# Seven block products for the up projection of MLP groups 2 to 4, and weight sums made in a memory scratch

## The chip, the cores and the metric

One core of a Trainium2 chip runs the kernel. The metric is the device time of one execution in microseconds (us). Its engines are TensorE (PE), which multiplies matrices and loads their stationary side (PEld); VectorE (DVE); ScalarE (ACT); GpSimd (POOL); and SyncE (SP), which here only issues transfers (DMA).

## The reference

One decoder layer on 512 tokens of width 1024. Three branches (a short convolution, a gated linear recurrence, attention into 256 memory tokens) are gated, merged, projected and added to the input; then comes the MLP that this change is about. All in float32:

```
x = layer_norm(ALPHA * x + mixed, ln1_g, ln1_b)
h = square(relu(x @ w_up))                                       # 512 x 4096
x = layer_norm(ALPHA * x + h @ w_down, ln2_g, ln2_b)             # w_up 1024 x 4096, w_down 4096 x 1024
```

## The kernel before

Every product of float32 operands is made of three matmuls (`three`, lines 1767 to 1771): each operand is split into a high part, a rounded copy that ScalarE makes, and a low part, the difference, that VectorE makes (`low_of`, line 1069); then high by high, high by low and low by high are added in a bank. Weights come in slabs of 1 MB (128 x 2048 floats), which SP loads. A slab's high part goes to one of four slots of `w_hi` and its low part to `w_lo`; `slab_hi` and `slab_lo` count them, and TensorE waits for `slab_lo` before it uses a slab.

The MLP works in 4 groups of 1024 hidden features. In a group, TensorE first makes 8 up tiles (`up_tile`) of 128 features by 512 tokens, each from all 8 row blocks of x. ScalarE takes a tile out of its bank with relu and square in its two token halves, and VectorE makes from a pair of tiles the operands of the down projection. That one is a 2 x 2 block product (2 blocks of 256 tokens, 2 blocks of hidden features, 2 blocks of outputs) done in seven products instead of eight. The products m1 to m7 multiply sums of blocks of h (the forms, `h_forms`, `form_hi`, `form_lo`) by blocks of w_down or sums of them. VectorE makes those sums (`sum_of`, line 1591) in `raw_a`, `raw_b` and `raw_c`, parts of the tensor `small`. Each product has two rows, for 128 of the 256 tokens, of 12 matmuls of 512 columns. The products m1, m6, m7 and m4 accumulate one after the other in one pair of banks and m5 and m3 in another; after each of them VectorE adds the bank as it then stands to the residual (`down_add`), and the next product of the bank waits for that (`down_ready`).

In front of the MLP the gates of branches 2 and 3 already use seven products with columns of 256 tokens (`seven_product`, `SEVEN`, with the sums in `gate_a`, `gate_b`, `gate_c`), with a ring of three slots. `gate_a` lies in the memory of the fourth slot of `w_hi`, `gate_b` in that of `w_lo`.

Each engine works through an order written out by hand: `mlp`, `seven_gate` and `plain_gate` on ScalarE and VectorE, the list of loads on SP. GpSimd does little: in each of the two projection halves it splits the memory keys and values of that half (lines 613 to 615), then it clears `merged` (line 633), scales the residual (line 637) and shares in the last normalization. It issues no transfer. Each of its instructions waits for those ahead of it.

Of the kernel before, what the change touches and what calls it, by code (L numbers as in the profile page):

```python
# [24 lines left out]
P = 128  # L25
T = 512
# [28 lines left out]
S_MLP, N_MLP = S_OUT + 4, 11  # L55
# [21 lines left out]
UP_SLABS = 4  # L77
# [5 lines left out]

SHARED = ((2, 0), (2, 1), (3, 0), (3, 1), (0, 0))
# [3 lines left out]
LAST_ROWS = (("m3", 0), ("m2", 0), ("m3", 1), ("m2", 1), ("m7", 0), ("m4", 0), ("m7", 1), ("m4", 1))  # L88


def made(g, name, r):

    at = 2 * PRODUCTS.index(name) + r
    if g == G_MLP - 1 and (name, r) in LAST_ROWS:
        at = 2 * len(PRODUCTS) - len(LAST_ROWS) + LAST_ROWS.index((name, r))
    return 2 * len(PRODUCTS) * g + at + 1


SUMS = ("m5", "m6", "m7", "m4")


def aside(g, name):

    return g == G_MLP - 1 and name == "m2"
# [39 lines left out]
def down_bank(g, name):  # L144
    return 2 if g == G_MLP - 1 and name == "m4" else DOWN_BANK[name]


def down_slab(g, name):
    return S_MLP + g * N_MLP + UP_SLABS + PRODUCTS.index(name)

# [34 lines left out]
def build(nc, x, mem, lower_bounds, w_in, conv_w, hg_norm_w, w_mem_k, w_mem_v, w_branch, b_gate, w_o,  # L185
          ln1_g, ln1_b, w_up, w_down, ln2_g, ln2_b, out):
    ds = bass.ds
    with ExitStack() as ctx:
# [49 lines left out]
        h_forms = two[:, 4:6, :].rearrange("p a (b t) -> p (a b) t", t=T // 2)[:, 0:7, :]  # L238
# [19 lines left out]
        form_of = dict(m7=gate_a[:, 0:1024], m6=gate_a[:, 1024:2048], m5=gate_b[:, 0:1024], m3=gate_b[:, 1024:2048])  # L258
        small = sb("small", [P, 9 * 1024])
# [18 lines left out]
        raw_a = small[:, 0:SLAB]  # L278
        raw_b = small[:, SLAB:2 * SLAB]
        raw_c = small[:, 2 * SLAB:3 * SLAB]  # L280
        late = small[:, 8192:9216].rearrange("p (c t) -> p c t", t=256)
        early = two[:, 4, :].rearrange("p (c t) -> p c t", t=256)
        h_kept = small[:, 8192:9216].rearrange("p (j t) -> p j t", j=PAIRS)
        aside_hi, aside_lo = (t[:, 0:PAIRS, :].rearrange("p k c -> p (k c)") for t in (x_hi, x_lo))
# [51 lines left out]
        a_landed, b_landed = sem("a_landed"), sem("b_landed")  # L336
        c_landed, sums_made = sem("c_landed"), sem("sums_made")
        up_done, up_read = sem("up_done"), sem("up_read")
        h_squared, form_step, forms_made = sem("h_squared"), sem("form_step"), sem("forms_made")
        forms_hi, forms_ready = sem("forms_hi"), sem("forms_ready")  # L340
        kept_hi, kept_ready = sem("kept_hi"), sem("kept_ready")
        down_done, down_read = sem("down_done"), sem("down_read")
# [23 lines left out]

        def main_of(eng, rnd, t):

            eng.wait_ge(tile_done, rnd * MAIN + (t + 1))
            return bank[t % MAIN]  # L370
# [19 lines left out]
        wdn = w_down[0].rearrange("(k two p) c -> p two k c", two=2, p=P)  # L390

        def down_block(g, k, n):

            return wdn[:, k - 1, g * PAIRS:(g + 1) * PAIRS, (n - 1) * WID:n * WID]
# [14 lines left out]

        def direct_slab(g, d):  # L410

            return S_MLP + g * N_MLP + d if d < UP_SLABS else down_slab(g, "m2")

        @block.sync
        def _(sp):
# [116 lines left out]
            sp.wait_ge(gate_done, seven_done(2, "m6", 1))  # L532
            par_load(2, ln2_g)
            par_load(3, ln2_b)
            def direct(g, d, src, k):

                n = R_MLP + 5 * g + d
                if n < R_MLP + 2:
                    sp.wait_ge(slab_lo, S_MLP - 2 + d + 1)
                else:  # L540
                    before = 5 * g + d - 2
                    sp.wait_ge(slab_lo, direct_slab(before // 5, before % 5) + 1)
                sp.dma_start(raw[:, n % 2, :].rearrange("p (k c) -> p k c", k=k), src).then_inc(slab_landed[n % 2], 16)

            def up_load(g, j):
                direct(g, j, wup[:, :, g * D + j * 256:g * D + (j + 1) * 256], KD)

            for g in range(G_MLP):
                up_load(g, 0)
                up_load(g, 1)  # L550
                if g == 0:
                    sp.wait_ge(merged_split, KD)
                else:
                    sp.wait_ge(slab_lo, down_slab(g - 1, "m4") + 1)
                sp.dma_start(as_block(raw_a), down_block(g, 1, 1)).then_inc(a_landed, 16)
                if g:
                    sp.wait_ge(sums_made, 4 * g)
                sp.dma_start(as_block(raw_b), down_block(g, 2, 2)).then_inc(b_landed, 16)
                if g == 0:
                    sp.wait_ge(x1_ready, 2 * TB)  # L560
                else:
                    sp.wait_ge(slab_lo, down_slab(g - 1, "m7") + 1)
                sp.dma_start(as_block(raw_c), down_block(g, 1, 2)).then_inc(c_landed, 16)
                up_load(g, 2)
                up_load(g, 3)
                direct(g, 4, down_block(g, 2, 1), PAIRS)
# [17 lines left out]
        def _(pool):  # L584
# [25 lines left out]

            for half in range(2):
# [40 lines left out]
        def _(act):  # L652
# [282 lines left out]

# [17 lines left out]
            def split(s, src):  # L953
                act.activation(w_hi[:, (s - S_MLP) % 4, :], src, ACT.Copy).then_inc(slab_hi, 1)  # L954
# [1279 lines left out]
```

## Time and profile before

| what | us |
|---|---|
| median of three runs | 821.65 (821.57 to 821.92) |
| the profiled execution, its own time | 821.65 |
| its span, first to last instruction | 819.9 |
| granted TensorE clock, mean of the span | 0.997 |
| TensorE matmul busy | 809.6 |
| VectorE busy | 552.2 |
| ScalarE busy | 373.2 |
| GpSimd busy | 32.7 |
| moved by DMA | 87.64 MB |

A matmul's record begins when it enters the array and overlaps the next ones, so the distance between two starts is what one costs, and its duration is longer. The start of a weight slab's use can be told by the operand names: x_hi in an up tile, y_hi (where the forms lie) in a down row, x_forms in the gates' products.

### The profile page before, as it was taken

Reading aid. Unit: us, or ns where it says so; the run is one execution under the profiler, and the core shown is the slowest. Engines: PE = TensorE matmul, PEld = TensorE weight load, DVE = VectorE, ACT = ScalarE, POOL = GpSimd, SP = SyncE. Lnnn points to the kernel's source line nnn. Section 1 sums busy time; section 2 is a strip of 40 time slices with the busy share of each in tenths; the row PEclk is TensorE's granted clock in tenths of the full one; section 3 lists DMA queues with packets and bytes.
Section 4 is the critical chain, followed back from the end, with each engine's and each line's share of the span. In section 5 each row is a group of like instructions: output and inputs, shape, how many; then the busy total and the mean of one; then the engine's idle time right before and its main releaser. Section 6 shows DMA issues by size and latency. Waiting matters only on the chain.

```text
span 819.9 us, 10644 instructions
## 1 busy us (share of the span) xinstructions
PE 809.6 (99%) x4347; PEld 699.2 (85%) x4347; DVE 552.2 (67%) x612; ACT 373.2 (46%) x435; POOL 32.7 (4%) x40
## 2 busy tenths in 40 slices
PE   8999999999999999999999999999999999999995
PEld 8889888899888889989988899888888888888884
DVE  4647655477358628778567676985588568856887
ACT  5559324493435324443453036643554355435532
POOL 1100100000001000000000010000000000000006
PEclk9999999999999999999999999999999999999998
DMA  9641313313120730620547116028102710270002
GB/s 309 205 155 52 103 52 102 102 51 102 51 78 26 255 103 1 223 86 1 207 153 255 53 51 207 1 75 288 48 1 81 278 52 1 90 270 1 1 0 104
DMA packets 64207, 87.64 MB, mean 107 GB/s; under 512 B 1661, under 2 KB 43686, under 8 KB 64166
## 3 DMA queue, kind: packets, MB, share of 16 engines
q1 hardware_dynamic: 64166, 87.06, 31.4%
q8 instruction: 30, 0.49, 0.2%
q14 instruction: 11, 0.09, 0.0%
HBM read 84.96 MB, written 2.10 MB: 106 GB/s over the span
## 4 chain that ended last, share of the span: by engine, by line
PE 98%; DVE 1%; DMA 1%; issue 0%; SPq 0%; DVEq 0%
PE bank L1769 31%; PE bank L1771 31%; PE bank L1770 31%; DMA two<-in_mem_dram 1%; PE bank L1796 0%; PE bank L1985 0%; PE bank L1935 0%; PE bank L2105 0%; PE bank L1906 0%; PE bank L1988 0%; PE bank L1973 0%; PE bank L1937 0%; DVE smx L1637 0%; PE bank L1942 0%; DVE two L1631 0%
## 5 line engine op out<-in xcount | busy, mean ns | idle before, releaser
L1769 PE MATMUL bank<-x_hi,w_hi 128*128 128x512 f32 (+1 forms) x672 | 245.7, 366 | 0.0
L1770 PE MATMUL bank<-x_lo,w_hi 128*128 128x512 f32 (+1 forms) x672 | 244.6, 364 | 0.0
L1771 PE MATMUL bank<-x_hi,w_lo 128*128 128x512 f32 (+1 forms) x672 | 244.5, 364 | 0.0
L1771 PEld LDWEIGHTS bank<-x_hi,w_lo 128*128 128x128 f32 x672 | 126.8, 189 | 20.1
L1769 PEld LDWEIGHTS bank<-x_hi,w_hi 128*128 128x128 f32 x672 | 126.8, 189 | 19.7
L1770 PEld LDWEIGHTS bank<-x_lo,w_hi 128*128 128x128 f32 x672 | 126.9, 189 | 19.6
L1769 PE MATMUL bank<-w_hi,y_hi 128*128 128x512 f32 x296 | 115.5, 390 | 0.0
L1771 PE MATMUL bank<-w_hi,y_lo 128*128 128x512 f32 x296 | 115.2, 389 | 0.0
L1770 PE MATMUL bank<-w_lo,y_hi 128*128 128x512 f32 x296 | 115.2, 389 | 0.0
L1070 DVE TENSOR_TENSOR w_lo<-raw,w_hi 128x2048 fp32r<-128x2048 f32 (+2 forms) x35 | 71.5, 2046 | 36.2 <-ACT w_hi L954 26.3
L1771 PEld LDWEIGHTS bank<-w_hi,y_lo 128*128 128x128 f32 x296 | 55.6, 188 | 11.6
L1770 PEld LDWEIGHTS bank<-w_lo,y_hi 128*128 128x128 f32 x296 | 55.6, 188 | 11.4
L1769 PEld LDWEIGHTS bank<-w_hi,y_hi 128*128 128x128 f32 x296 | 55.6, 188 | 11.3
L1070 DVE TENSOR_TENSOR w_lo<-small,w_hi 128x2048 fp32r<-128x2048 f32 (+1 forms) x28 | 59.9, 2138 | 3.6 <-ACT w_hi L680 1.7
L954 ACT ACTIVATE w_hi<-raw 128x2048 fp32r<-128x2048 f32 x17 | 32.6, 1918 | 63.6 <-PE bank L1771 35.4
L1065 DVE TENSOR_TENSOR w_lo<-raw,w_hi 128x2048 fp32r<-128x2048 f32 x22 | 50.4, 2296 | 16.0 <-ACT w_hi L659 15.8
L954 ACT ACTIVATE w_hi<-small 128x2048 fp32r<-128x2048 f32 x24 | 45.7, 1906 | 10.2 <-PE bank L1771 10.2
L1631 DVE TENSOR_TENSOR two<-two,bank 128x512 f32<-128x512 f32 x56 | 38.3, 684 | 15.8 <-PE bank L1771 10.2
L659 ACT ACTIVATE w_hi<-raw 128x2048 fp32r<-128x2048 f32 x22 | 42.2, 1919 | 12.4 <-DMA raw<-in_w_branch_dram 11.4
L1769 PE MATMUL bank<-y_hi,w_hi 128*128 128x512 f32 (+1 forms) x128 | 46.9, 367 | 0.0
L1770 PE MATMUL bank<-y_lo,w_hi 128*128 128x512 f32 (+1 forms) x128 | 46.4, 363 | 0.0
L1771 PE MATMUL bank<-y_hi,w_lo 128*128 128x512 f32 (+1 forms) x128 | 46.4, 362 | 0.0
(252 smaller groups left out, 1145.3 us busy)
## 6 DMA issues: line engine op xcount, KB each, us to landing
raw<-in_w_in_dram SPq DMA_DIRECT2D x22, 1024.0 KB, 5.1
raw<-in_w_up_dram SPq DMA_DIRECT2D x16, 1024.0 KB, 6.9
small<-in_w_down_dram SPq DMA_DIRECT2D x12, 1024.0 KB, 7.8
raw<-in_w_branch_dram SPq DMA_DIRECT2D x6, 1024.0 KB, 5.1
two<-in_x_dram SPq DMA_DIRECT2D x4, 1024.0 KB, 9.2
raw<-in_w_o_dram SPq DMA_DIRECT2D x4, 1024.0 KB, 5.1
raw<-in_w_down_dram SPq DMA_DIRECT2D x4, 1024.0 KB, 4.7
small<-in_w_mem_v_dram SPq DMA_DIRECT2D x4, 512.0 KB, 10.9
```

Of the source, the lines that this page charges most:

```text
L659: act.activation(w_hi[:, slot, :], raw[:, r, :], ACT.Copy).then_inc(slab_hi, 1)
L954: act.activation(w_hi[:, (s - S_MLP) % 4, :], src, ACT.Copy).then_inc(slab_hi, 1)
L1065: dve.tensor_tensor(w_lo[:, slot, :], raw[:, r, :], w_hi[:, slot, :].bitcast(F32), ALU.subtract)\
L1070: return dve.tensor_tensor(dst, src, high.bitcast(F32), ALU.subtract)
L1631: dve.tensor_tensor(z, z, bank[down_bank(g, name) + r], op).then_inc(down_read, 1)
L1769: pe.matmul(dst, a[0], b[0], start=first, stop=False, skip_group_check=goes_on)
L1770: pe.matmul(dst, a[0], b[1], start=False, stop=False, skip_group_check=goes_on)
L1771: return pe.matmul(dst, a[1], b[0], start=False, stop=last, skip_group_check=goes_on)
```

## The change

The up projection of groups 2 to 4 becomes seven block products as well: 2 blocks of x's features, 2 blocks of hidden features, 2 blocks of 256 tokens. Group 1 keeps its plain tiles, and during it VectorE makes the forms of x (`x1_forms`) once for all groups. Every up product is 48 matmuls of 256 columns in a pair of banks. ScalarE copies m1, m5 and m6 out, VectorE adds m3, m2 and m7 to the copies, and relu and square follow on whole blocks of h. The blocks of h are 1024 columns wide (`h11`, `h12`, `h21`, `h22`), and the forms of the down projection are made on them with one operation each (`form`) instead of in four column parts. The down products run in the order m1, m2, m5, m6, m3, m7, m4.

VectorE makes no weight sums any more. GpSimd copies four blocks of the weights into a scratch in memory (`kept`) for each of seven jobs (the down projection of each group, the up projection of groups 2 to 4), and then adds block to block there with accumulating transfers, four per job. SP loads the sums like weights. The first four jobs are begun and summed in the projection halves, behind GpSimd's splitting of the memory values, and the other three after the clearing of `merged`. All MLP slabs run in one ring of three slots (`mlp_load`, `mlp_hi`, `mlp_lo`), whose third raw buffer is `gate_a`; a group has 14 slabs (the first 11). The rows of the second normalization are loaded in the last group instead of ahead of the MLP.

```diff
+ROWS = ("m1", "m2", "m5", "m6", "m3", "m7", "m4")
+ROW_BANK = dict(m1=6, m6=6, m7=6, m4=6, m2=4, m5=0, m3=0)
+UP_BANK = dict(m1=0, m6=0, m7=0, m4=0, m5=2, m3=2, m2=4)
+SUM_STEPS = (("m5", "m7"), ("m7", "m6"), ("m6", "m5"), ("m4", "m6"))
+JOBS = (("down", 0), ("up", 1), ("down", 1), ("up", 2), ("down", 2), ("up", 3), ("down", 3))
 # SyncE
+            def mlp_load(n, src, k):
+                if n < 2:
+                    sp.wait_ge(slab_lo, S_MLP - 2 + n + 1)
+                elif n == 2:
+                    sp.wait_ge(tile_done, mlp_round(0) * MAIN)
+                else:
+                    sp.wait_ge(slab_lo, S_MLP + n - 3 + 1)
...
+            def product_load(kind, g, name):
+                n = up_slab(g, name) if kind == "up" else down_slab(g, name)
+                if name in SUMS:
+                    j = JOBS.index((kind, g))
+                    sp.wait_ge(kept_made[j], KEPT)
+                    mlp_load(n, kept_sum(j, name), PAIRS)
...
 # GpSimd
+            def begin_sums(jobs):
+                for j in jobs:
+                    kind, g = JOBS[j]
+                    for name in SUMS:
+                        k, n = SUM_BEGINS[name]
+                        pool.dma_start(kept_sum(j, name), up_block(g, k, n) if kind == "up" else down_block(g, k, n))\
+                            .then_inc(kept_made[j], 16)
+            def make_sums(jobs):
+                for n, (to, other) in enumerate(SUM_STEPS):
+                    for j in jobs:
+                        pool.wait_ge(kept_made[j], 16 * (len(SUMS) + n))
+                        pool.dma_start(kept_sum(j, to), kept_sum(j, other), accum_op=ALU.add, max_dma_last_dim=8192)\
+                            .then_inc(kept_made[j], 16)
...
                 parts(mem_v[:, :, half * 256:(half + 1) * 256], mv_hi, mv_lo, 2 * half + 2, vhalf_ready)
+                if half == 0:
+                    pool.wait_ge(x_landed[1], 16)
+                    pool.wait_ge(value_landed[3], 16)
+                    begin_sums(range(0, 4))
+                else:
+                    make_sums(range(0, 4))
             pool.wait_ge(branch_split, 8)
             pool.memset(merged, 0.0).then_inc(merge_done, 1)
+            begin_sums(range(4, 7))
+            make_sums(range(4, 7))
 # ScalarE
+            def mlp_hi(n):
...
+                elif n > 2:
+                    act.wait_ge(mlp_done, slab_done(n - 3, 1))
+                mlp_landed(act, n)
+                act.activation(w_hi[:, n % 3, :], mlp_raw(n), ACT.Copy).then_inc(slab_hi, 1)
 # VectorE
+            def down(g):
+                last = g == G_MLP - 1
+                form(g, "m5")
+                form(g, "m7")
+                mlp_lo(down_slab(g, "m5"))
+                form_to_lo(g, "m5")
+                form(g, "m6")
+                form(g, "m3")
+                mlp_lo(down_slab(g, "m6"))
+                form_to_lo(g, "m6")
+                down_add(g, "m1", 0)
+                down_add(g, "m1", 1)
+                form_to_lo(g, "m3")
+                mlp_lo(down_slab(g, "m3"))
+                down_add(g, "m5", 0)
+                down_add(g, "m5", 1)
+                mlp_lo(down_slab(g, "m7"))
+                form_to_lo(g, "m7")
+                for r in range(2):
+                    down_add(g, "m2", r)
...
                 down_add(g, "m6", 0)
                 down_add(g, "m6", 1)
+                mlp_lo(down_slab(g, "m4"))
+                form_to_lo(g, "m4")
...
                 down_add(g, "m3", 0)
                 down_add(g, "m3", 1)
+                down_add(g, "m7", 0)
+                mlp_lo(up_slab(g + 1, "m1"))
+                down_add(g, "m7", 1)
+                mlp_lo(up_slab(g + 1, "m5"))
+                down_add(g, "m4", 0)
+                down_add(g, "m4", 1)
 # TensorE
+            def up_product(g, name):
+                n = up_slab(g, name)
...
+                for p in range(2):
+                    up_ready(g, name, p)
+                    for c in range(2):
+                        dst = bank[UP_BANK[name] + p][:, c * 256:(c + 1) * 256]
+                        for k in range(PAIRS):
+                            if name in X1_SLOT:
+                                b = both(x1_form_hi, x1_form_lo, ALL, X1_SLOT[name], slice(k * 256, (k + 1) * 256))
+                            else:
+                                row = k if name == "m1" else PAIRS + k
+                                b = both(x_hi, x_lo, ALL, row, slice(0, 256) if name == "m4" else slice(256, 512))
+                            mm = three(dst, w_part(n % 3, k * WID + (2 * p + c) * P, P), b,
+                                       opens and c == 0 and k == 0, k == PAIRS - 1, not opens or c == 1)
+                    mm.then_inc(mlp_done, 1)
```

## Rows read from the trace of the kernel before

**Rows 1.** The page's first and fourth part: busy time by engine, the chain by engine.
```profile
PE 809.6 (99%) x4347; PEld 699.2 (85%) x4347; DVE 552.2 (67%) x612; ACT 373.2 (46%) x435; POOL 32.7 (4%) x40
...
PE 98%; DVE 1%; DMA 1%; issue 0%; SPq 0%; DVEq 0%
```
**Rows 2.** The waits of PE: who waited <- for whom: total, times, longest.
```profile
PE bank L1803 <- POOL ident L594: 1.5, 1, 1.5
```
**Rows 3.** Window of a group: busy time (instructions), PEclk, DMA share, GB/s.
```profile
core 0: us, PE busy (x) PEld busy (x) DVE busy (x) ACT busy (x) POOL busy (x), PEclk, DMA share, GB/s
566.70:648.30 81.60, 81.60 (x362) 67.59 (x361) 56.73 (x50) 36.63 (x36) 0.00 (x0) 1.00 0.31 103
```
**Rows 4.** Timeline of ACT, first tile of groups 2 and 3: start, duration, instruction.
```profile
572.33 0.60 ACT L997 ACTIVATE two<-bank 128x512 f32<-128x512 f32 x1 [3.04 <-PE bank L1771]
...
653.93 0.60 ACT L997 ACTIVATE two<-bank 128x512 f32<-128x512 f32 x1 [2.09 <-PE bank L1771]
```
**Rows 5.** Timeline of PE: first matmul of group 1's down projection, of group 2.
```profile
528.61 0.39 PE L1769 MATMUL bank<-w_hi,y_hi 128*128 128x512 f32 x1
...
566.69 0.39 PE L1769 MATMUL bank<-x_hi,w_hi 128*128 128x512 f32 x1
```
**Rows 6.** Timeline of PE: first matmul of a gate product, and of what follows.
```profile
341.27 0.28 PE L1769 MATMUL bank<-x_forms_a,w_hi 128*128 128x256 f32 x1
...
347.03 0.40 PE L1769 MATMUL bank<-y_hi,w_hi 128*128 128x512 f32 x1
```
**Rows 7.** Timelines of DVE and ACT in group 1's down projection.
```profile
540.79 2.29 DVE L1070 TENSOR_TENSOR w_lo<-raw,w_hi 128x2048 fp32r<-128x2048 f32 x1
542.99 1.22 DVE L1070 TENSOR_TENSOR y_lo<-small,y_hi 128x1024 fp32r<-128x1024 f32 x1
544.13 0.68 DVE L1631 TENSOR_TENSOR two<-two,bank 128x512 f32<-128x512 f32 x1
...
538.33 1.92 ACT L954 ACTIVATE w_hi<-raw 128x2048 fp32r<-128x2048 f32 x1 [4.42 <-PE bank L1771]
540.16 1.04 ACT L1026 ACTIVATE y_hi<-small 128x1024 fp32r<-128x1024 f32 x1
541.10 1.90 ACT L954 ACTIVATE w_hi<-small 128x2048 fp32r<-128x2048 f32 x1
```
**Rows 8.** Timeline of POOL: splits of the memory values and keys, clearing, scaling.
```profile
36.44 1.29 POOL L615 TENSOR_TENSOR y_lo<-small,y_hi 128x512 fp32r<-128x512 f32 x1
60.02 0.61 POOL L613 CAST y_hi<-small 128x512 fp32r<-128x512 f32 x1 [22.29 <-PE bank L1771]
...
253.91 3.53 POOL L633 MEMSET small<- 128x4096 f32 x1 [164.33 <-DVE y_lo L1070]
459.61 1.05 POOL L637 TENSOR_SCALAR two<-two 128x1024 f32<-128x1024 f32 x1 [202.17 <-PE bank L2105]
```
**Rows 9.** Timelines: second half's scores on PE, first gate sigmoid on ACT, branch tiles.
```profile
162.94 0.28 PE L1769 MATMUL bank<-y_hi 128*128 128x256 f32 x1
...
257.48 1.49 ACT L860 ACTIVATE two<-bank,par 128x512 f32<-128x512 f32 x2 [1.38 <-POOL small L633]
...
268.95 0.39 PE L1769 MATMUL bank<-y_hi,w_hi 128*128 128x512 f32 x1
```
**Rows 10.** Window of gate_c's load, then timelines of SP, DVE and PE on it.
```profile
301.80:307.00 5.20, 5.20 (x24) 4.32 (x23) 1.38 (x2) 0.68 (x1) 0.00 (x0) 1.00 0.63 205
...
301.79 0.92 SPq L493 DMA_DIRECT2D gate_c<-in_w_in_dram  x2
...
308.64 2.35 DVE L1347 TENSOR_TENSOR gate_a<-gate_a,gate_c 128x1024 f32<-128x1024 f32 x2
320.89 2.29 DVE L1070 TENSOR_TENSOR w_lo<-gate_a,w_hi 128x2048 fp32r<-128x2048 f32 x1 [2.04 <-ACT w_hi L837]
...
323.99 0.28 PE L1769 MATMUL bank<-x_forms_b,w_hi 128*128 128x256 f32 x1
```
**Rows 11.** The page's sixth part: issues, KB each, median us from issue to landing.
```profile
raw<-in_w_in_dram SPq DMA_DIRECT2D x22, 1024.0 KB, 5.1
...
small<-in_w_down_dram SPq DMA_DIRECT2D x12, 1024.0 KB, 7.8
```
**Rows 12.** Timeline of PE: the last matmul.
```profile
811.27 0.39 PE L1771 MATMUL bank<-w_hi,y_lo 128*128 128x512 f32 x1
```

More of the change, by code:

```diff
@@ new lines, in _ @@
+            for j in range(4):
+                at = (j // 2) * (DFF // 2) + (j % 2) * 256
+                mlp_load(j, wup[:, :, at:at + 256], KD)
+            for g in range(G_MLP):
+                if g:
+                    for name in PRODUCTS:
+                        product_load("up", g, name)
+                for name in ROWS:
+                    if g == G_MLP - 1 and name == "m6":
+                        sp.wait_ge(mlp_done, slab_done(up_slab(g, "m3"), 1))
+                        par_load(2, ln2_g)
+                        par_load(3, ln2_b)
+                    product_load("down", g, name)
@@ L1053, in _, with mark, marked, activated @@
-            for g in range(G_MLP):
-                mlp(g)
+            steps = [0]
+            def mark(ins):
+                ins.then_inc(act_step, 1)
+                steps[0] += 1
+            def marked():
+                act.wait_ge(act_step, steps[0])
+            def activated(z):
+                mark(act.activation(z, z, ACT.Relu))
+                marked()
+                return act.activation(z, z, ACT.Square)
+            def form_to_hi(g, name):
+                act.activation(form_hi[:, FORM_OF[name], :], h_of[name], ACT.Copy).then_inc(forms_hi, 1)
@@ new lines, in down @@
+            def down(g):
[18 more added lines that the diff above has]
+                    down_add(g, "m2", r)
+                    if last:
+                        half_stats(g, "m2", r)
@@ L1743, in last_rows @@
                 norm_two(0, 1)
-            for g in range(G_MLP):
-                mlp(g, g == G_MLP - 1)
+            plain_up()
+            down(0)
+            for g in range(1, G_MLP):
+                seven_up(g)
+                down(g)
         @block.tensor
@@ L2158, in down_part @@
[L2158 to L2168 removed]
+                feature_part(bank[u], slice(T // 2, T), u // 2, u % 2).then_inc(mlp_done, 1)
@@ new lines, in row @@
+            def row(g, name, r):
+                n = down_slab(g, name)
+                slab(S_MLP + n)
+                pe.wait_ge(forms_ready, form_ready(g, name))
+                down_ready(g, name, r)
+                opens = name in DOWN_OPENS or down_bank(g, name) != ROW_BANK[name]
+                for j in range(PAIRS):
+                    mm = three(bank[down_bank(g, name) + r],
+                               both(form_hi, form_lo, ALL, FORM_OF[name], slice(j * 256 + r * P, j * 256 + (r + 1) * P)),
+                               w_part(n % 3, j * WID, WID), opens and j == 0, j == PAIRS - 1, not opens)
+                mm.then_inc(mlp_done, 1)
@@ L2214 @@
+            for g in range(G_MLP):
+                if g:
+                    for name in PRODUCTS:
+                        up_product(g, name)
+                last = g == G_MLP - 1
+                for name in ROWS[0:4 if last else 7]:
+                    for r in range(2):
+                        row(g, name, r)
+                if last:
+                    for name, r in LAST_ROWS:
+                        row(g, name, r)
 _INS = ["x", "mem", "lower_bounds", "w_in", "conv_w", "hg_norm_w", "w_mem_k", "w_mem_v", "w_branch", "b_gate",
```

568 lines of the change are left out of this document (284 added, 284 removed).

## The prediction

> **What bounds the kernel now.** I read the page's first part, then the chain, then TensorE's waits. TensorE is busy 99% of the span and the chain of waits is 98% TensorE [rows 1]; its longest wait on anything is 1.5 us, at the start [rows 2]. So in the MLP the time is the number of matmuls by their spacing, as long as no operand is late. One MLP group lasts 81.6 us from one group's first activation to the next [rows 4], at granted clock 1.00, the 2.4 GHz level, with VectorE at 57 of 82 us and ScalarE at 37 [rows 3]. Spacing, not duration, is the price, because matmuls overlap: the 168 matmuls of 512 columns of a down projection begin at 528.61 and the next group's first at 566.69, 38.08/168 = 0.2267 us each [rows 5]. A product of 48 matmuls of 256 columns in the gate stage runs from 341.27 to 347.03, 0.120 us each [rows 6]: half the columns cost 53%, not 50%.
>
> **TensorE's part of the change.** Before, an up projection is 8 tiles of 8 row blocks by 3 = 192 matmuls of 512 columns, 192 x 0.2267 = 43.5 us (43.5 + 38.1 = the 81.6 of the group). After, seven products of 2 x 2 x 4 x 3 = 48 matmuls of 256 columns are 336 x 0.120 = 40.3 us. Each of groups 2 to 4 gives 3.2 us, together 9.6 us. Were the 256-column matmul exactly half, it would be 16.3; the trace shows 0.120 for the same three-matmul pattern, so I take that. The first group and all down projections keep their matmul counts.
>
> **VectorE and ScalarE.** A group loses 4 weight sums, the 16 short form operations of 256 columns and their wide roundings; it gains 3 slab splits, 6 additions out of the banks, 4 forms of 1024 columns and 7 roundings of single forms. Prices, start to next start: a slab's low part 2.20 (540.79 to 542.99), a form's 1.14 (542.99 to 544.13), a bank addition 0.6 alone and 0.73 when the next waits for it (own 0.68 plus the signal), a slab's high part on ScalarE 1.84, a form's 0.95 [rows 7]. VectorE's group: 14 x 2.2 + 4 x 1.14 + 7 x 1.14 + 6 x 0.6 + 14 x 0.7 = 57 us of 78.4; ScalarE's 14 x 1.84 + some 20 us = 46. Neither is the bound by sum; what matters is order.
> The tight place is the first group's down projection, where VectorE must do 4 forms, 5 form splits, 5 slab splits, then additions, within 7 rows of 5.44 us, and where the next product of a bank accumulates onto it, so may start only when it was added. Walking VectorE's queue with these prices from TensorE's first row m1 at 528.6: m2's form is split by 532.7 (needed 534.0); m5's forms and split by 538.5 (needed 539.5); m6's by 544.2, then m1's first addition by 544.8, while m6 wants the bank at 544.9; m3's and m7's operands come 1 to 2 us ahead; m7 wants m6's bank at 555.8 and m6's addition ends at 555.7. Then m7's form and slab, m4's slab and form, two m3 additions and m7's end at 561.8, while m4 wants the bank at 561.3: 0.5 us late, and 0.1 on its second half. In groups 2 to 4 the forms m2, m1 and two slabs are split during the up products, and the same walk keeps at least 1.4 us at every row, except the last m4, whose form comes 0.5 us late because the block statistics of the last group stand ahead of it. Sum of stalls 1.1 us; lower end 0, upper end 3.5 (0.15 more on each of the 16 operations ahead of that m4, 2.4). In the up products the smallest margin is 1.9 us (m4's bank after m7's addition).
> **Slabs with a ring of three.** A slab's slot is free when the product three before is done, which leaves two products, 11 us, for ScalarE's 1.9 and VectorE's 2.3; loads are issued a product earlier still. A landing may take up to 11 us without moving the walk; the down loads took 7.8 [rows 11]. All sums are read as one more load, so SP's waits on kept_made cost nothing if GpSimd was done by then; the first sum is wanted at about 510.
> **The end.** The same last rows and normalization follow the last matmul at 811.27 [rows 12]: unchanged. The ln2 rows land later, under group 4: nothing.
>
> **GpSimd and the memory scratch.** This adds 28 copies of 1 MB and 28 accumulations of 1 MB, 56 transfers against the 87 MB moved now. Nothing in the trace is a memory-to-memory or accumulating transfer, so I bound them. Below: the gate's 1 MB moved in 0.63 of 5.2 us = 3.3 us of full use of the DMA engines [rows 10], so 3.3 for a copy and for an accumulation. Above: 7.8 for a copy, the slow kind of load [rows 11], and 9.9 for an accumulation that reads two and writes one (3 x 3.3). I take 5.5 and 6.5. What GpSimd has to do between them: it issues 16 copies after its work at 36.4 to 37.7, and its next work, the rounding of the second half's keys, stands at 60.0 [rows 8], behind 16 x 5.5 = 88 us if the ring lets few transfers stand, so at 126. TensorE wants it at 162.9 [rows 9]: free, up to 7.7 per copy. Then 16 accumulations, each of whose steps waits for the step before: 126 + 16 x 6.5 = 230. Its clearing of `merged` is at 253.9 for 3.5 us, ScalarE starts on it at 257.5, and the bank is wanted by the branch tiles at 268.95 [rows 8, 9]: some 7 to 10 us of cover beyond 253.9. The second batch, 12 + 12 after 257.4, ends at 257 + 66 + 78 = 401, before the residual scaling at 459.6 [rows 8], which the additions want only at 544. So the cost here is 0.
> **Transfers beside each other.** Copies run at 302, when SP issues the two 0.5 MB loads of gate_c. They land about 306.7; the sum that reads them starts at 308.64, and the chain sum, high part, low part, next sum ends at 323.2 (320.89 + 2.29) for a product that starts at 323.99 [rows 10]. So a landing late by 2 + 0.8 = 2.8 us is hidden. If the load shares the engines half and half it is 3.3 us late: 0.5 us on the path. Lower end 0, upper end 6 (three times its time: 6.6 + 2 for the queue - 2.8). Elsewhere in the projections slabs are split some 15 us ahead.
> The trace shows only one busy queue and so no sharing. The Trainium skill, "DMA: Bandwidth & Descriptors", section "Queues, rings and completion order", says that each DMA engine alternates between queues that have work, one packet at a time. By that rule small rows beside 8 KB accumulations get less than half of the bytes, which is the second rival.
>
> **Sum.** The profiled execution took 821.65: 819.9 span and 1.75 around it; the median is 821.65 too. 821.65 - 9.6 + 1.1 + 0.5 = 813.65, so 813.7.
>
> **Rivals.** (1) *GpSimd's queue is late* (slower). If an accumulation takes 9.9 and a copy 5.5, GpSimd reaches the clearing at 126 + 158 = 284 instead of 254; less the 8 us of cover TensorE stands 22 us in the first gate tiles: 836. It decides from (262 - 126)/16 = 8.5 us per accumulation; break-even with before at 9.0. For: a step needs its predecessor landed, and two reads and a write are 9.9 at the measured rate. Against: four sums are under way at once, and rows of 8 KB are large. With copies of 7.7 the limit is 6.1.
> (2) *SP's loads starve beside GpSimd's transfers.* One packet of each in turn: a load takes its own 5.1 us [rows 11] once or twice more, 10 to 15. ScalarE's in-order queue stands on its high part, and the sigmoids and exponentials behind it. I price it at 6 us at gate_c instead of 0.5: 819; with the same in each half's projections, up to 825. For: 56 MB more; against: 15 us of cover there.
> (3) *VectorE's order stalls every group*, not just the first: 3.5 us instead of 1.1, and 1.5 for each other group: 820.6. Against: margins of 1.4 us in the walk.
>
> **How the numbers follow.** Forecast (812 to 816) 0.53; rival 2 0.18 (of which a fourth above 820); rival 3 0.05; rival 1 0.20; better than 812 (no stall at all, 812.05 less a little) 0.04. Faster by over 0.2% (below 820.0; 0.2% is about what a measurement of this kernel can tell from nothing): 0.72; within 0.05; slower 0.23. The range 811.6 to 822.5 takes in the bounds of the stalls (0 to 3.5) and of gate_c (0 to 6), and leaves out rival 1's 0.2. The likeliest case alone is 812.0 to 816.0.
>
> **What would show it.** Groups 2 to 4 spaced 78.4 us; 256-column matmuls of x1_form at 0.120; TensorE's wait before the first m4 row at about 0.5 us and none in up products; GpSimd's clearing still at 254, the accumulations' queue done before 430; gate_c landing 8 us after issue. Wrong if groups are spaced over 79.5, if TensorE waits behind the clearing of `merged`, or if ScalarE's high parts wait for DMA in the projections.

## The result, and the profile after

| | us |
|---|---|
| before, median of 4 runs | 821.78 (821.57 to 822.04) |
| after, median of 4 runs | 907.48 (905.74 to 909.93) |
| ratio | 1.104 [1.103, 1.106] |
| the profiled execution after, its own time; span | 909.93; 908.1 |
| forecast | 813.7, range 811.6 to 822.5 |

The change costs 10%, where a gain of 1% was forecast. The page of the changed kernel, its second to fourth part:

```profile
PE   9999999824699999996059999999999999999993
...
PEclk9999999957799999999579999999999999999997
DMA  9788679999222497799915440433555555565622
...
q1 hardware_dynamic: 58358, 109.08, 35.4%
q0 software_dynamic: 11648, 58.72, 24.9%
...
PE 64%; DVE 10%; DMA 9%; another core or an unknown queue 8%; issue 4%; ACT 4%; SPq 0%; DVEq 0%; ACTq 0%
```

Read the three strips together. From slice 22 on (each is 22.7 us) TensorE is full but for the tail; the MLP, all that the forecast calls gain, begins in slice 26. TensorE stands in slices 8 to 11 and 19 to 21, in the projections and the gates, where the change did not touch it, and in both places the DMA strip reads 9, from a slice ahead on. Queue q0, GpSimd's, is new. The chain was 98% TensorE [rows 1] and is 64% now. The waits of the changed kernel (who waited <- for whom: total, times, longest) name the links:

```profile
ACT w_hi L741 <- DMA raw<-in_w_in_dram: 61.4, 5, 30.4
...
ACT w_hi L919 <- DMA gate_a<-in_w_in_dram: 44.7, 1, 44.7
...
PE bank L1917 <- DVE w_lo L1191: 39.8, 3, 37.3
...
PE bank L1917 <- DVE y_lo L1191: 21.7, 1, 21.7
...
PE bank L2054 <- DVE small L1299: 20.9, 1, 20.9
```

TensorE's three long waits, 37.3, 21.7 and 20.9 us, go back through VectorE to ScalarE's high part of a slab, and that waits for a transfer. The chain's 8% for "another core or an unknown queue" are two of these waits: its pieces of 25.48 us from 196.90 and 44.66 us from 412.89 end where ScalarE, in its own timeline, stops waiting for `raw` and `gate_a`. Why the transfer is late is in the list of issues (median us from issue to landing) and in the DMA view of the stretch 150 to 198 us, in the middle of GpSimd's first batch of sums:

```profile
kept<-kept POOLq DMA_DIRECT2D x28, 1024.0 KB, 15.8
raw<-in_w_in_dram SPq DMA_DIRECT2D x22, 1024.0 KB, 6.9
...
kept<-in_w_down_dram POOLq DMA_DIRECT2D x16, 1024.0 KB, 5.8
```
```profile
q0 software_dynamic: 1290, 9.41, 94.1%
q1 hardware_dynamic: 1290, 1.30, 9.7%
...
raw<-in_w_in_dram SPq DMA_DIRECT2D x2, 1024.0 KB, 55.4
```

In 48 us both queues moved the same number of packets, 1290. GpSimd's are rows of 8 KB, SP's are rows of 1 KB, so one got 9.41 MB and the other 1.30. A packet of q0 took 0.941 x 48 x 16 / 1290 = 0.56 us and one of q1 0.097 x 48 x 16 / 1290 = 0.058. A slab of 1 MB in rows of 1 KB is 1024 packets, 64 for each of the 16 engines, so beside the sums it takes an estimated 64 x 0.62 = 40 us; alone it took 5.1 [rows 11]. The chain shows one such load, from its issue to the high part that waits for it:

```profile
139.87 43.63 DMA raw<-in_w_in_dram
```

The median of the whole page, 6.9, hides this: most loads had no sum beside them.

The window with the first hole (columns as in [rows 3]), then the timelines of GpSimd, SP and TensorE:

```profile
160.00:200.00 40.00, 19.14 (x97) 16.33 (x97) 12.54 (x22) 13.09 (x26) 6.57 (x8) 0.77 1.04 223
```
```profile
132.09 0.71 POOL L687 CAST y_hi<-small 128x512 fp32r<-128x512 f32 x1
...
136.90 2.65 POOL L682 DMA_DIRECT2D kept<-kept  x3
...
150.54 0.81 POOL L682 DMA_DIRECT2D kept<-kept  x1 [4.58 <-issue]
155.93 0.81 POOL L682 DMA_DIRECT2D kept<-kept  x1 [4.58 <-issue]
...
209.66 0.82 POOL L682 DMA_DIRECT2D kept<-kept  x1 [4.45 <-issue]
301.17 3.53 POOL L713 MEMSET small<- 128x4096 f32 x1 [90.69 <-DVE y_lo L1191]
```
```profile
139.87 98.65 SPq L480 DMA_DIRECT2D raw<-in_w_in_dram  x5
```
```profile
461.92 0.58 PE L1917 MATMUL bank<-x_hi,w_hi 128*128 128x256 f32 x1 [37.27 <-DVE w_lo L1191]
...
462.94 0.41 PE L1918 MATMUL bank<-x_lo,w_hi 128*128 128x256 f32 x1
```

GpSimd's queue is not late: it splits the keys at 132 (forecast 126), issues a sum every 5.4 us (forecast 6.5) and the last of the first batch at 210. Its clearing of `merged` waits 90.7 us for the others. The issues of SP's five loads from 139.87 on stretch over 98.65 us. TensorE does half of its work in the window, at a mean granted clock of 0.77. When it starts again, at 461.92 behind the last hole of 37 us, the 256-column matmuls from 462.30 to 462.94 begin 0.21 us apart instead of 0.12; the granted clock from 461 to 465 us is 0.50, the 1.2 GHz level, and from 465.06 on the spacing is 0.12 again. Against the same kernel without its sums (e1, span 817.9, TensorE busy 800.7) TensorE's idle time is 83.0 us longer (908.1 - 807.9 = 100.2 against 17.2) and the same 4779 matmuls are busy 7.2 us longer, of which the lower clock is the visible cause: together the 90.2 us between the two spans.

### The profile page after: what moved, and what is told of

It is laid out like the page before. It is cut to its first block, busy times and chain, and to the rows that moved or that the text cites. A ratio compares the mean times of both kernels' runs of the same rounds, so it can differ in the third digit from the quotient of the medians.

```text
span 908.1 us, 11640 instructions
## 1 busy us (share of the span) xinstructions
PE 807.9 (89%) x4779; PEld 717.8 (79%) x4779; DVE 558.8 (62%) x595; ACT 400.3 (44%) x453; POOL 77.1 (8%) x96
## 4 chain that ended last, share of the span: by engine, by line
PE 64%; DVE 10%; DMA 9%; another core or an unknown queue 8%; issue 4%; ACT 4%; SPq 0%; DVEq 0%; ACTq 0%
PE bank L1917 20%; PE bank L1918 20%; PE bank L1919 20%; DMA raw<-in_w_in_dram 5%; DMA raw<-in_w_branch_dram 3%; DVE w_lo L1191 3%; DVE two L1761 2%; DVE y_lo L1191 1%; DMA gate_c<-in_w_in_dram 1%; ACT w_hi L919 1%; DMA two<-in_mem_dram 1%; DVE gate_b L1730 1%; DVE two L1730 1%; DVE gate_a L1476 0%
## 5 line engine op out<-in xcount | busy, mean ns | idle before, releaser
L1917 PE MATMUL bank<-x_hi,w_hi 128*128 128x512 f32 (+1 forms) x624 | 212.6, 341 | 37.3 <-DVE w_lo L1191 37.3
L1918 PE MATMUL bank<-x_lo,w_hi 128*128 128x512 f32 (+1 forms) x624 | 211.2, 339 | 0.0
L1919 PE MATMUL bank<-x_hi,w_lo 128*128 128x512 f32 (+1 forms) x624 | 211.1, 338 | 0.0
L1191 DVE TENSOR_TENSOR w_lo<-raw,w_hi 128x2048 fp32r<-128x2048 f32 (+2 forms) x52 | 110.3, 2123 | 49.2 <-ACT w_hi L1025 28.0
L1191 DVE TENSOR_TENSOR w_lo<-gate_a,w_hi 128x2048 fp32r<-128x2048 f32 x25 | 57.2, 2289 | 66.0 <-ACT w_hi L919 48.2
L1025 ACT ACTIVATE w_hi<-raw 128x2048 fp32r<-128x2048 f32 x36 | 68.7, 1912 | 51.7 <-PE bank L1919 51.5
L741 ACT ACTIVATE w_hi<-raw 128x2048 fp32r<-128x2048 f32 x22 | 42.2, 1918 | 74.5 <-DMA raw<-in_w_in_dram 61.4
L1918 PE MATMUL bank<-x_forms_b,w_hi 128*128 128x256 f32 x256 | 72.4, 283 | 0.0
L1917 PE MATMUL bank<-x_form_hi,w_hi 128*128 128x256 f32 x192 | 54.3, 283 | 0.0
L1919 PE MATMUL bank<-x_form_hi,w_lo 128*128 128x256 f32 x192 | 54.3, 283 | 0.0
L1918 PEld LDWEIGHTS bank<-x_forms_b,w_hi 128*128 128x128 f32 x256 | 49.1, 192 | 0.0
## 6 DMA issues: line engine op xcount, KB each, us to landing
kept<-kept POOLq DMA_DIRECT2D x28, 1024.0 KB, 15.8
```

Of the source, the lines that this page charges most:

```text
L741: act.activation(w_hi[:, slot, :], raw[:, r, :], ACT.Copy).then_inc(slab_hi, 1)
L1025: act.activation(w_hi[:, n % 3, :], mlp_raw(n), ACT.Copy).then_inc(slab_hi, 1)
L1191: return dve.tensor_tensor(dst, src, high.bitcast(F32), ALU.subtract)
L1917: pe.matmul(dst, a[0], b[0], start=first, stop=False, skip_group_check=goes_on)
L1918: pe.matmul(dst, a[0], b[1], start=False, stop=False, skip_group_check=goes_on)
L1919: return pe.matmul(dst, a[1], b[0], start=False, stop=last, skip_group_check=goes_on)
```

## The experiments

All ratios are to the kernel before, run on the same chip; they are estimates of their own and differ a little from the quotient of two medians (e8: 0.9950, e4: 1.0164).

| | what | us (range) | ratio |
|---|---|---|---|
| e1 | after, without the 28 sums | 819.56 (818.81 to 820.08) | 0.9973 [0.9963, 0.9982] |
| e2 | after, without scratch | 819.42 (818.75 to 820.72) | 0.9972 [0.9961, 0.9983] |
| e3 | sums in 2 KB packets | 882.86 (877.26 to 887.23) | 1.0722 [1.0686, 1.0757] |
| e4 | one sum under way at a time | 835.13 (824.92 to 837.74) | 1.0179 [1.0162, 1.0196] |
| e5 | e4, clearing ahead of the later sums | 819.86 (819.08 to 820.26) | 0.9977 [0.9968, 0.9986] |
| e6 | e3, clearing ahead of the later sums | 819.99 (819.05 to 821.98) | 0.9980 [0.9971, 0.9989] |
| e7 | before, plus the 56 transfers | 907.37 (904.63 to 909.09) | 1.1037 [1.1016, 1.1057] |
| e8 | e5, last group rebalanced | 817.62 (817.34 to 818.66) | 0.9956 [0.9942, 0.9969] |
| e9 | e8, four shared half blocks | 818.19 (818.05 to 818.50) | 0.9956 [0.9942, 0.9969] |
| e10 | e8, GpSimd's share left out | 814.25 (813.84 to 814.69) | 0.9906 [0.9891, 0.9921] |
| e11 | e5, two sums under way | 880.18 (876.43 to 880.89) | 1.0698 [1.0677, 1.0720] |

**e1, e2: take the sums, then the whole scratch, away.** e1 keeps the copies and leaves the block sums uncomputed; e2 has no GpSimd transfer, and SP loads one block where a sum is wanted.

```diff
 # e1
-KEPT = 16 * (len(SUMS) + len(SUM_STEPS))
+KEPT = 16 * len(SUMS)
...
-                for n, (to, other) in enumerate(SUM_STEPS):
+                for n, (to, other) in enumerate(()):
 # e2
-                    j = JOBS.index((kind, g))
-                    sp.wait_ge(kept_made[j], KEPT)
-                    mlp_load(n, kept_sum(j, name), PAIRS)
+                    at = SUM_BEGINS[name]
+                    mlp_load(n, up_block(g, *at) if kind == "up" else down_block(g, *at), PAIRS)
...
-                for j in jobs:
+                for j in ():
...
-                for n, (to, other) in enumerate(SUM_STEPS):
+                for n, (to, other) in enumerate(()):
```


> All 28 copies into the scratch stay, the 28 accumulating transfers are left out (SP reads the copied blocks, so the sums are not formed). Theory A (each DMA engine takes one packet of each queue in turn, and an accumulation's packet of 8 KB holds it 0.63 us against 0.06 us for a load's packet of 1 KB, so loads starve only while accumulations run): the waits of 37.3, 21.7 and 20.9 us vanish, 814 to 818, with a small wait left at gate_c beside the copies. Theory B (the bytes of the scratch traffic fill the engines, whatever their packets): the copies are 28 of 112 MB read or written, a quarter of the 86 us stays, about 830 to 835. Theory C (GpSimd's own queue is late): the keys are still split at 132, no change from that, 814.

> No scratch at all: SP loads one block of the weights where the changed kernel loads a sum (so the sums are left out), GpSimd issues no transfer. All theories: this is TensorE's, VectorE's and ScalarE's part alone, so it measures the terms 9.6 gained and 1.1 of stalls: 813.1, between 812 and 815. If it stands above 817, the arithmetic part of my sum was wrong too.

The 28 accumulations cost 907.5 - 819.6 = 88 us, the 28 copies nothing that can be measured (819.56 against 819.42). The copies' packets differ: from 60 to 90 us of the changed kernel GpSimd's queue moved 1445 of them, 5.59 MB, so under 4 KB each, for 51.9% of the engines' time, 0.17 us a packet, and SP's two loads there landed in 5.5 us. Yet neither e1 nor e2 reached the 813 of the sum; by e2's own expectation a time above 817 says that its arithmetic part was wrong too. e1's TensorE, at the borders of the groups' up and down parts and at its last matmul:

```profile
686.94 0.40 PE L1917 MATMUL bank<-w_hi,y_hi 128*128 128x512 f32 x1
...
725.05 0.28 PE L1917 MATMUL bank<-x_hi,w_hi 128*128 128x256 f32 x1
...
765.36 0.40 PE L1917 MATMUL bank<-w_hi,y_hi 128*128 128x512 f32 x1
...
804.17 0.39 PE L1919 MATMUL bank<-w_hi,y_lo 128*128 128x512 f32 x1
```

Up 765.36 - 725.05 = 40.31 us, down 725.05 - 686.94 = 38.11: the group of 78.42 us that was forecast. The last matmul is 7.1 us ahead of before [rows 12], but the span only 2.0: some 5 us are lost behind it. e8 to e10 take that up.

**e7: the transfers alone.** The kernel before, with GpSimd's copies and sums in the same places of its queue, into a scratch that nobody reads:

```diff
...
+                if half == 0:
...
+                    begin_sums(range(0, 4))
+                else:
+                    make_sums(range(0, 4))
...
             pool.wait_ge(branch_split, 8)
             pool.memset(merged, 0.0).then_inc(merge_done, 1)
+            begin_sums(range(4, 7))
+            make_sums(range(4, 7))
```


> The kernel before with nothing changed but GpSimd's 28 copies and 28 accumulations, issued in the same places of its queue as in the changed kernel, into a scratch that nobody reads. It computes everything as before. Theory A (the accumulations starve SP's loads of slabs with 1 KB and 2 KB rows in the projections and gates): it loses what the changed kernel loses against the one without accumulations, 88 us: 821.7 + 88 = 905 to 913. Rival D (part of the 88 us is the changed kernel's own: SP's waits for the sums, the ring of three slots, the late second normalization rows): 880 or less.

907.37 - 821.77 = 85.6 us: nearly all of the 88 is reproduced without any new product, ring or order on the other engines. Rival D (880 or less) falls.

**e3, e4: smaller packets, or pauses.** e3 makes each sum as two transfers of 64 rows of the array in packets of 2 KB; e4 keeps 8 KB and lets GpSimd wait for each landing.

```diff
 # e3
-                        pool.dma_start(kept_sum(j, to), kept_sum(j, other), accum_op=ALU.add, max_dma_last_dim=8192)\
+                        for e in (slice(0, 64), slice(64, 128)):
+                            pool.dma_start(kept_sum(j, to)[e], kept_sum(j, other)[e], accum_op=ALU.add,
+                                           max_dma_last_dim=2048).then_inc(kept_made[j], 16)
 # e4, behind each accumulation
+                        pool.wait_ge(kept_made[j], 16 * (len(SUMS) + n + 1))
```


> The same accumulations and bytes, but in rows of 2 KB instead of 8 KB, each as two transfers of 64 partitions. Theory A: a load's packet now waits for a packet a quarter as long (0.15 to 0.2 us), so a load of 64 packets per engine lands in 14 to 17 us instead of about 40; the three long waits shrink to 20 us or less together, 815 to 840. Theory B: bytes are the same, 900 to 915. Theory C: GpSimd issues twice as many transfers and is later, above 910.

> Rows of 8 KB as before, but GpSimd waits until an accumulation has landed before it issues the next, so only one is under way. Theory A: between two of them the engines serve the loads alone for about 2 us, in which 0.6 MB pass; a load lands in 8 to 14 us, and the accumulations take 7 to 8 us each, so the first batch ends at 136 + 16 x 7.5 = 256 and the clearing of merged is at most some us late: 815 to 835. Theory B: same bytes in little more time, above 890. Theory C: GpSimd is held longer, above 910.

e4 got back 72 of 88 us, the upper edge of what the packet theory (A) gave; e3 only 25, at 883 far outside its 815 to 840. e4's executions differ: the profiled one took 824.92, the others 833.56 to 837.74. The DMA view of the same 48 us (packets, MB, share of 16 engines; then an issue's landing) in e4, then in e3:

```profile
q0 software_dynamic: 839, 6.22, 68.0%
q1 hardware_dynamic: 4160, 4.19, 26.2%
...
raw<-in_w_in_dram SPq DMA_DIRECT2D x4, 1024.0 KB, 7.4
```
```profile
q0 software_dynamic: 2070, 3.98, 48.4%
q1 hardware_dynamic: 4160, 4.19, 27.8%
...
raw<-in_w_in_dram SPq DMA_DIRECT2D x4, 1024.0 KB, 5.4
```

In both, SP's four slabs of that stretch arrive, in 7.4 and 5.4 us: the loads no longer starve. The reason is not the same alone: e4's GpSimd queue pauses (68.0%) between packets of 8 KB, and e3's has packets of 2 KB, 0.484 x 48 x 16 / 2070 = 0.18 us each, but is busy only 48.4% of the time too. Beside an unbroken row of such packets a load would take an estimated 64 x (0.18 + 0.06) = 15 us, three times what it took. So e3 does not tell smaller packets from pauses. What remains of the loss is another mechanism. e3's waits and its timeline of GpSimd, then e4's:

```profile
ACT two L943 <- POOL small L714: 76.6, 1, 76.6
```
```profile
329.43 3.85 POOL L714 MEMSET small<- 128x4096 f32 x1
```
```profile
248.84 0.83 POOL L682 DMA_DIRECT2D kept<-kept  x1 [7.32 <-DMA kept<-kept]
257.70 0.82 POOL L682 DMA_DIRECT2D kept<-kept  x1 [8.03 <-DMA kept<-kept]
265.29 3.52 POOL L714 MEMSET small<- 128x4096 f32 x1 [6.77 <-DMA kept<-kept]
```

This is the forecast's rival 1, GpSimd's clearing behind its sums, with its place right: at 329 and at 265 instead of 254, once a sum costs 11.8 us ((329.4 - 141.3)/16 in e3) or 8.3 ((265.3 - 132.5)/16 in e4). The profile of e4 is that of the 824.92 execution; TensorE's waits behind the clearing are 0.2 and 2.8 us there, and no trace shows the other 10 us of the median. In the changed kernel it did not happen, because there a sum was issued every 5.4 us.

**e5, e6: the same two with the clearing in time.** GpSimd makes the sums of two jobs ahead of the clearing, of two behind the later copies, and of three behind the residual scaling.

```diff
-                    make_sums(range(0, 4))
+                    make_sums(range(0, 2))
...
             begin_sums(range(4, 7))
-            make_sums(range(4, 7))
+            make_sums(range(2, 4))
...
+            make_sums(range(4, 7))
```


> As e4 (one accumulation under way at a time), but GpSimd makes only the sums of the first two jobs before it clears `merged`, those of the next two after the 12 copies, and those of the last three after the residual scaling. Theory A with the queue (accumulations under way starve SP's loads packet by packet, and what e4 still lost is GpSimd's clearing at 265.3 instead of 254): the clearing is back at 254 to 256, no hole in front of the gate tiles, and the time is that of the kernel without a scratch plus at most the 0.5 us at gate_c: 819.5 to 821. Rival B (it is the 59 MB more that the DMA engines move): the bytes are unchanged, so e4's 835 stays, 830 or more. In either the 5 us that are missing at the end stay.

> As e3 (accumulations in packets of 2 KB, not waited for one by one), with GpSimd's work in the order of e5. e3 took 883 and its profile has one hole of 65 us, in front of the first gate tile, behind GpSimd's clearing of `merged`, while its loads landed in 7.5 us. Theory: with packets of 2 KB the loads no longer starve, and the 65 us was GpSimd's queue, as 16 sums took 12.5 us each; with the clearing in time 820 to 823. Rival: even 2 KB packets starve the loads and the hole moves elsewhere: 850 or more.

819.86 and 819.99, both as expected, with all 28 sums made and used. e5's timeline of GpSimd:

```profile
254.71 3.53 POOL L714 MEMSET small<- 128x4096 f32 x1 [48.43 <-DVE y_lo L1193]
```

So e4's last 15 us and e3's last 63 came from the order of GpSimd's queue. The bytes are the same 168 MB in e3 to e6 as in the changed kernel: the theory that the added traffic itself costs falls too.

**e11: how many under way.** As e5, but GpSimd waits for the sum before the one just issued.

```diff
-                        pool.wait_ge(kept_made[j], 16 * (len(SUMS) + n + 1))
+                        if before:
+                            pool.wait_ge(*before[-1])
+                        before.append((kept_made[j], 16 * (len(SUMS) + n + 1)))
```


> As e5, but two accumulations may be under way: GpSimd waits for the landing of the one before the last. Theory A says that SP's loads come through in the pauses of GpSimd's queue, which is empty for about 2 us of every 8 when one accumulation is under way; with two it is never empty, every load packet of 1 KB waits for one of 8 KB, and a load takes about 41 us while sums are made: 8 sums of 5.5 us starve the second half's projection for 44 us (one hole of some 20 us), 8 more the gate (another): 845 to 870. Rival I (it takes a full ring of descriptors, three under way, to hold the loads back): 820 to 825.

880.2, some 10 us beyond what I had expected, on the side of theory A: the rival's 820 to 825 is out. e11's DMA view from 150 to 170 us:

```profile
q0 software_dynamic: 525, 3.91, 93.7%
q1 hardware_dynamic: 524, 0.54, 9.6%
```

Two under way already leave no pause, and the packets go one for one again. Where I was short: the third batch, three jobs in the MLP, opened a hole of 14 us there too.

**e8, e9, e10: the end.** In e8 GpSimd, idle until the last normalization, makes the low part of the last slab, and VectorE adds and measures m3's first row ahead of m4's form. e9 also gives VectorE the fifth half block of the normalization. e10 leaves GpSimd's part of the normalization (scale and shift of five half blocks) out.

```diff
 # GpSimd (e8)
+            n = down_slab(G_MLP - 1, "m4")
+            pool.wait_ge(slab_hi, S_MLP + n + 1)
+            pool.wait_ge(slab_lo, S_MLP + n)
+            pool.tensor_tensor(w_lo[:, n % 3, :], mlp_raw(n), w_hi[:, n % 3, :].bitcast(F32), ALU.subtract)\
+                .then_inc(slab_lo, 1)
...
 # VectorE (e8)
-                mlp_lo(down_slab(g, "m4"))
-                form_to_lo(g, "m4")
                 if last:
                     last_rows(g)
                     return
+                mlp_lo(down_slab(g, "m4"))
+                form_to_lo(g, "m4")
...
                 complete("m3", 0)
+                form_to_lo(g, "m4")
 # e9
-SHARED = ((2, 0), (2, 1), (3, 0), (3, 1), (0, 0))
+SHARED = ((2, 0), (2, 1), (3, 0), (3, 1))
...
+                own_begin(2, 0, 0)
                 own_begin(2, 0, 1)
...
+                own_end(2, 0, 0)
                 own_end(2, 0, 1)
 # e10
...
-                pool.tensor_tensor(resid[:, b, part], resid[:, b, part], ln_par[:, 2, part], ALU.mult)\
...
+                pool.memset(eps[:, 2 + n:3 + n], 0.0).then_inc(shared_ready, 1)
```


> As e5, and in the last group GpSimd, idle there, splits m4's slab (VectorE's 2.29 us), and VectorE adds and measures m3's first row before it splits m4's form. Theory E (the 5 us that the kernel without a scratch misses stand after the last matmul because VectorE has no idle time from 768 to the end and gives GpSimd its normalization work at 800.2, 4.7 us ahead of the last matmul, when before it was 11.3 us ahead): GpSimd starts its share about 3 us earlier, the wait of 0.8 us before the last m4 goes, and the time is 2.5 to 4 us under e5: 815.5 to 817.5. Rival F (the tail is set by something else, the stores or the last norm, or GpSimd's split slows VectorE by as much): within 0.7 us of e5.

> As e8, but GpSimd normalizes four half blocks instead of five at the end; VectorE does the fifth, with two operations of about 0.7 us each. In e8's profile VectorE's last pair of operations took 3.07 us while GpSimd worked, where before the same pair took 1.42 after GpSimd had ended, and the pair behind it 2.22 instead of 1.42. Theory G (part of the tail is VectorE and GpSimd slowing each other): GpSimd ends 2.9 us earlier and VectorE begins its last pairs 2.0 us later, so the first pair goes at half speed for at most half of its time: the 2.0 us are won back within 0.7: 817 to 818.5. Rival H (VectorE's operations are slow for another reason): 2 us slower than e8, 819.5 or more.

> As e8, but GpSimd leaves out its five half blocks of the last normalization (scale and shift by the second layer norm's parameters); their stores go out all the same. Theory G: VectorE's last two pairs take 1.42 us each as in the kernel before, its first single operations beside GpSimd 1.0 to 1.2 us become 0.7: 3.0 us less, 814 to 815. Rival H: unchanged, 817 to 818.

e8 is 2.2 us under e5, a little less than expected, and the fastest version that computes everything: 4.2 us under before by the medians, 0.44% by the ratio. Its two edits, the slab and the order, were not tried apart. GpSimd's share begins at 797.16, 2.3 us earlier than in e1. The tails in the timelines of GpSimd (its first shared operation) and VectorE (its last two pairs): of before, of e1, of e8, and VectorE's of e10.

```profile
799.99 1.30 POOL L644 TENSOR_TENSOR two<-two,small 128x512 f32<-128x512 f32 x1 [306.24 <-ACT two L1048]
...
814.45 1.42 DVE L1664 SCALAR_TENSOR_TENSOR two<-two,mv,small 128x512 f32<-128x512 f32 x2
...
815.97 1.42 DVE L1669 SCALAR_TENSOR_TENSOR two<-two,lnw,small 128x512 f32<-128x512 f32 x2
```
```profile
799.43 1.29 POOL L726 TENSOR_TENSOR two<-two,small 128x512 f32<-128x512 f32 x1 [304.87 <-ACT two L1152]
...
809.88 3.08 DVE L1794 SCALAR_TENSOR_TENSOR two<-two,mv,small 128x512 f32<-128x512 f32 x2
...
813.07 2.22 DVE L1799 SCALAR_TENSOR_TENSOR two<-two,lnw,small 128x512 f32<-128x512 f32 x2
```
```profile
789.12 4.62 POOL L727 TENSOR_TENSOR w_lo<-raw,w_hi 128x2048 fp32r<-128x2048 f32 x1 [180.84 <-ACT w_hi L1032]
797.16 1.29 POOL L733 TENSOR_TENSOR two<-two,small 128x512 f32<-128x512 f32 x1 [3.42 <-ACT two L1159]
...
807.63 3.07 DVE L1801 SCALAR_TENSOR_TENSOR two<-two,mv,small 128x512 f32<-128x512 f32 x2
```
```profile
807.44 1.42 DVE L1797 SCALAR_TENSOR_TENSOR two<-two,mv,small 128x512 f32<-128x512 f32 x2
...
808.97 1.41 DVE L1802 SCALAR_TENSOR_TENSOR two<-two,lnw,small 128x512 f32<-128x512 f32 x2
```

Before, GpSimd got its work 11.3 us ahead of the last matmul (799.99, 811.27) and was done when VectorE came to its last pairs. In e1 it gets it only 4.7 us ahead (799.43, 804.17), so the last pairs run beside it, 3.08 and 2.22 us instead of 1.42 each. The 5.1 us are: 2.5 until the first pair begins (5.71 us behind the last matmul, before 3.18), 1.7 in the first pair, 0.8 in the second, 0.1 behind. e10, where GpSimd does nothing beside them, has both pairs back at 1.42 and is 3.4 us faster than e8; e9, where they run behind GpSimd's end, pays the same by two slowed pairs ahead of them and ends 0.6 us behind e8, no clear difference from it (their ranges overlap) and inside what was expected; rival H's 819.5 or more is out. Theory G stands. So does theory E, that VectorE comes late to m3 because its work is packed there: e8's 2.2 us are beyond rival F's 0.7. Windows of e2 over the last group's down part:

```profile
770.00:780.00 10.00, 10.00 (x46) 8.27 (x45) 9.97 (x8) 8.40 (x7) 0.00 (x0) 1.00 0.37 112
780.00:790.00 10.00, 10.00 (x46) 8.29 (x45) 9.70 (x10) 3.93 (x3) 0.00 (x0) 1.00 0.27 100
790.00:800.00 10.00, 9.36 (x42) 7.46 (x41) 9.30 (x13) 1.48 (x6) 0.00 (x0) 1.00 0.00 0
```

VectorE is busy 29 of these 30 us, while TensorE had 6 rows left behind m6 to cover it and no longer 8.

## Why the prediction was wrong

**TensorE's part was right.** 40.31 us for an up part (40.3), 78.42 for a group (78.4). The stalls of the walk came at the two places named: in e1 the first group's down part is 0.7 us longer (forecast 0.6), the last one's 0.95 (forecast 0.5), the others' 0. gate_c beside the copies cost 0.46 us (forecast 0.5).

**GpSimd's queue was right for this kernel.** A copy held it 6.2 us ((131.47 - 37.95)/15 between the first issue and the last; forecast 5.5) and a sum 5.4 (6.5), and rival 1 did not come. It was to decide from 8.5 us per sum. e4 at 8.3 in its profile lost 3 us there, and e3 at 11.8 lost 64.5: the threshold was about right. (With copies of 7.7 the limit comes to 6.3, not 6.1; no copy was that slow in the mean.)

**"Transfers beside each other" is the step that failed.** It put 0.5 us at gate_c and nothing elsewhere; the runs showed 88 us. The forecast knew that loads might get one packet in turn with GpSimd's, and made it a rival: "a load takes its own 5.1 us once or twice more, 10 to 15". That counts a packet as a packet. The size was in the diff, 8192 bytes per packet of a sum, and SP's rows are 1 KB. The measured terms: 64 packets per engine, each behind one of 0.56 us, 40 us per load instead of 10 to 15. It could be bounded from rows: at [rows 10]'s 3.3 us of full use per MB, 8 KB on one of 16 engines take 0.41 us, so 64 x 0.41 + 5 = 31 us. The step also priced the loads at one place, gate_c and 6 us, and trusted "some 15 us" of cover elsewhere. Against 40 us per load the cover is gone for as long as sums are under way: some 85 us of the second half's projections (136.9 to about 223) and some 70 of the gates (378.8 to about 450). From 137 to 218 us SP's queue moved 2.02 MB, two loads, where before it moved 6.29 MB, six; 88 us were lost. One of the forecast's own signs of being wrong came true: ScalarE's high parts waited for DMA in the projections, 61.4 us. The Trainium skill, "DMA: Bandwidth & Descriptors", section "Queues, rings and completion order", says that each DMA engine goes round its queues in turn, a packet from each. The trace agrees, 1290 packets against 1290, if a packet is what the profile counts: one row of 8 KB or of 1 KB. The same section of the Trainium skill puts several descriptors into a typical packet; for SP's rows the count here is one against one. The rule was cited in the forecast and its consequence, that shares go by size of packet, was drawn only as "less than half of the bytes", when it was 12% (1.30 of 10.71 MB).

**"The end: unchanged" failed too**, hidden behind the first error: +5.1 us. The same rows do follow the last matmul, but the forecast did not carry VectorE's walk on beyond TensorE's last stall. GpSimd's share begins with m3's first row, which VectorE reached late. Without sums the kernel would have come to 819.6, not 813.7: 821.65 - 9.6 + 1.7 + 0.5 + 0.3 for a later start + 5.1 = 819.65; e1's profiled execution took 819.72.

**The rivals.** Rival 2 named the mechanism and gave it at most 11 us (825) where it cost 88, a factor of eight. The range took its 6 us at gate_c in; the bounds named there add up to 821.55 (813.65 + 2.4 + 5.5), not 822.5. It held e1, e2, e5 and e6, but not the change.

## What to carry to other kernels

Before putting a transfer beside loads that something waits for, compare the two row sizes and not only the bytes: here the two queues got one packet each in turn, so rows of 8 KB beside rows of 1 KB left the loads a ninth of the bytes, and a tenth of the engines' time. Pauses between such transfers (one under way at a time) cured it, and so did packets of 2 KB in a queue that was busy half of the time, at the same number of bytes, but they make the issuing queue slower, and what stands behind them in it must be moved ahead. When an engine other than the bound has lost its idle time in the last stretch, walk its queue to the very end: what it hands on late is paid in full behind the last matmul.

## What the hardware showed that I had not expected

- An accumulation of 1 MB from memory to memory in packets of 8 KB: 5.4 us apart with three under way, landing 15.8 us after issue; 7.9 us from issue to landing with one under way (e4's median). Two halves in packets of 2 KB: 5.3 us each (e3's median), some 12 us per MB in the queue. More packets for the same bytes made the sum dearer; the loads came through (5.4 us), in e3 with the queue's pauses as well.
- A copy of 1 MB from memory to memory: 5.8 us from issue to landing. Beside the 28 copies TensorE waited for a load only once, 0.46 us at gate_c (e1).
- VectorE and GpSimd slow each other on operations with two operands from on-chip memory: VectorE's pair of 512-column operations 1.42 us alone, 3.07 beside GpSimd; GpSimd's multiplication 1.29 us alone and about 1.7 beside VectorE's. VectorE's additions with one operand from a bank were not slowed: 0.67 beside GpSimd (e8, at 805.95), 0.68 without (e10). The Trainium skill, "SBUF — State Buffer", section "Who interferes with whom", describes the port that the two engines share as a lock that one holds for its whole instruction. The trace agrees in size, 1.42 + 1.6; it does not show which of them waited for which.
- GpSimd made the low part of a 1 MB slab in 4.62 us beside a working VectorE, which needs 2.29 for it.
